# TensorE waits for its own last product at the column groups of four stages

## What is computed

```python
def swiglu(h, w_in, w_out):
    gate, up = jnp.split(h @ w_in, 2, axis=-1)
    return (jax.nn.silu(gate) * up) @ w_out

def sq_relu_mlp(u, w_up, w_down):
    return jnp.square(jax.nn.relu(u @ w_up)) @ w_down

for layer in range(2):
    x = x + 0.5 * swiglu(rmsnorm(x, ffn1_norm[layer]), ffn1_w_in[layer], ffn1_w_out[layer])
    ...
    x = x + 0.5 * swiglu(rmsnorm(x, ffn2_norm[layer]), ffn2_w_in[layer], ffn2_w_out[layer])
for i in range(4):
    ...
    h = h + rmsnorm_2(sq_relu_mlp(u, mlp_w_up[i], mlp_w_down[i]), norm_gains[i, 3])
```

## Time and profile before

| | |
|---|---|
| median of 3 runs | 2801.15 us (2799.4 to 2806.18) |
| the profiled execution | 2810.09 us |
| its span, first to last instruction | 2808.3 us |
| TensorE products / weight loads, share of the span | 96% / 93% |
| VectorE, ScalarE | 65%, 50% |
| mean share of the transfer engines' time | 48.8% |
| mean granted TensorE clock | 0.992 of full speed |

### The profile page before, as it was taken

The page is one execution under the profiler, slowest core; times in us unless marked ns, Lnnn a source line. Parts: engine busy times, 40 slices in busy tenths (PEclk is TensorE's granted clock), DMA queues, the critical chain, the costliest instruction groups (busy, mean ns, idle before and its releaser), DMA issues. The chain is left out here.

```text
span 2808.3 us, 49234 instructions
## 1 busy us (share of the span) xinstructions
PE 2706.5 (96%) x21106; PEld 2609.7 (93%) x21106; DVE 1817.8 (65%) x2364; ACT 1410.7 (50%) x1928; POOL 0.2 (0%) x4
## 2 busy tenths in 40 slices
PE   8999999999998899999999999989999899999998
PEld 8998999999987889999899999879988899989998
DVE  6658666656657746666656755967455685656764
ACT  5445654454466354545445465354454544446443
POOL 0000000000000000000000000000000000000000
PEclk9999999999999999999999999999999999999999
DMA  6554546555534234655544554135542465454463
GB/s 240 173 183 141 185 138 195 187 185 188 188 122 123 76 123 133 200 186 175 177 134 154 181 195 151 61 114 181 191 149 91 148 195 195 152 171 150 151 198 133
DMA packets 129865, 450.12 MB, mean 160 GB/s; under 512 B 20208, under 2 KB 21104, under 8 KB 129520
## 3 DMA queue, kind: packets, MB, share of 16 engines
q1 hardware_dynamic: 129504, 446.83, 48.8%
q10 hardware_dynamic: 144, 0.14, 0.0%
HBM read 445.48 MB, written 1.44 MB: 159 GB/s over the span
## 5 line engine op out<-in xcount | busy, mean ns | idle before, releaser
L266 PE MATMUL B<-R,WH 128*128 128x256 f32 x10432 | 2088.0, 283 | 37.6 <-DVE WL L980 23.4
L266 PEld LDWEIGHTS B<-R,WH 128*128 128x128 f32 x10432 | 1675.3, 189 | 57.1 <-DVE WL L980 25.0
L980 DVE TENSOR_TENSOR WL<-SL,WH 128x1024 fp32r<-128x1024 f32 x835 | 1010.4, 1223 | 755.0 <-ACT WH L2037 753.9
L266 PE MATMUL B<-R,WL 128*128 128x256 f32 x4480 | 1254.9, 280 | 0.0
L2037 ACT ACTIVATE WH<-SL 128x1024 fp32r<-128x1024 f32 x835 | 866.1, 1053 | 585.5 <-PE B L266 458.2
L266 PEld LDWEIGHTS B<-R,WL 128*128 128x128 f32 x4480 | 846.7, 189 | 0.0
L266 PE MATMUL B<-RB,WH 128*128 128x256 f32 x1984 | 555.5, 280 | 1.8 <-DVE WL L980 1.8
L266 PE MATMUL B<-RB,WL 128*128 128x256 f32 x1728 | 482.3, 279 | 0.0
L266 PEld LDWEIGHTS B<-RB,WH 128*128 128x128 f32 x1984 | 372.2, 188 | 2.5 <-DVE WL L980 2.2
L266 PEld LDWEIGHTS B<-RB,WL 128*128 128x128 f32 x1728 | 324.4, 188 | 0.0
L266 PE MATMUL B<-WH,R 128*128 128x512 f32 x480 | 159.2, 401 | 1.1 <-DVE WL L980 1.1
(11 more groups left out here) (287 smaller groups left out, 1583.0 us busy)
## 6 DMA issues: line engine op xcount, KB each, us to landing
SL<-in_w SPq DMA_DIRECT2D x835, 512.0 KB, 3.5
CP<-in_cp SPq DMA_DIRECT2D x5, 768.0 KB, 6.6
PG<-in_mem SPq DMA_DIRECT2D x1, 1024.0 KB, 7.1
PK<-in_pk SPq DMA_DIRECT2D x1, 594.5 KB, 7.1
XG<-in_xT SPq DMA_DIRECT2D x1, 512.0 KB, 7.7
out<-XG SPq DMA_DIRECT2D x1, 512.0 KB, 2.6
SL<-in_w SPq DMA_DIRECT2D x1, 384.0 KB, 3.5
XG<-in_xT SPq DMA_DIRECT2D x1, 256.0 KB, 6.1
```

What stands on the lines that cost most here:

```text
L266: return p.matmul(o, left, right, start=first, stop=final, skip_group_check=True)
L980: v.tensor_tensor(WL[t % NSPL][:, :], SL[t % NRAW][:, :], WH[t % NSPL][:, :].bitcast(F32), ALU.subtract).then_inc(s_lo, 1)
```

## The change

Two waits of TensorE for itself are added, nothing is taken away.

In f2.0.in (groups 1 to 21) and m0.up (groups 1 to 15), ahead of the group's first block, TensorE waits until `s_block` has reached the number of that block, i.e. until its own last product is done. In m0.up the first blocks of groups 1 and 2 are the second and third block of the stage.

In f1.1.in and f2.1.in (groups 1 to 21) it waits for the bank of the next small product, issues one more product of the group's weights (128 columns of them) with the first 16 + 2j columns of the activations into that bank, and waits for it on a semaphore of its own. What it writes is read by nobody, and the bank's turn isn't moved on.

```diff
+        own_mm = Tally(sem("s_own_mm"))
...
             def tile(st, j, k):
                 b = st.at(j, k)
+                if k == 0 and st.name in ("f2.0.in", "m0.up") and j:
+                    p.wait_ge(s_block, b)
                 if b == 0:
                     p.wait_ge(s_lo_first, 1)
                 elif b == 1 or b % 4 == 0:
...
             def multiply(st, j, k, xh, xl, lower=None):
                 hi, lo, at = tile(st, j, k)
+                if k == 0 and st.name in ("f1.1.in", "f2.1.in") and j:
+                    x = len(took)
+                    p.wait_ge(s_bank[4 + x % 3], x // 3)
+                    mm(BK[4 + x % 3][:, 0:16 + 2 * j], hi[:, at:at + 128], xh[:, 0:16 + 2 * j]).then_inc(own_mm.sem, own_mm.up())
+                    p.wait_ge(own_mm.sem, own_mm.n)
                 if k == 0 and st.used(j):
                     p.wait_ge(s_bank[st.bank(j)], st.used(j))
                 bk = BK[st.bank(j)]
```

## The result

The changed kernel takes 2834.49 us, the median of four runs (2829.59 to 2838.34), beside 2803.06 us for four runs of the kernel before (2799.4 to 2806.18): a ratio of 1.0112, with a 95% interval of 1.0089 to 1.0134. That is 31.4 us more, where the forecast was 24.6, and 8.8 us above the forecast time of 2825.7, inside the range of 2818 to 2840. The profiled execution of the changed kernel took 2829.59 us, 2827.8 of them its span.

The account below looks back on a forecast made before the run. TensorE, 96% busy, was taken to bound the kernel nearly everywhere. Thirty exposed waits (9.8 us) and 42 short products with waits (14.8 us) add 24.6 us to 2801.15, giving 2825.7 us, range 2818 to 2840.

Parts of the forecast that it names:

- The pure wait: In f2.0.in and m0.up, each exposed wait on s_block costs 0.326 us; 30 of them cost 9.8 us.
- the upper one: Upper bound for the signal from product end to weight load: 0.13 us, against 0.055 taken.
- The six hidden ones: Group 1 of f2.0.in and five waits in m0.up cost nothing, covered by other stalls; uncovered they cost 2.0 us.
- The short product: In f1.1.in and f2.1.in, each short product with its wait costs 0.352 us; 42 of them cost 14.8 us.
- four passes: If so narrow a product ran in four passes of 38 columns: 0.048 us more each, 2.0 us in all.
- The clock did not fall: Rival: the clock falls in the touched stages, giving 2847 or 2976 us; chance 0.07 of adding over 12 us.
- The weight load is held: Rival: TensorE loads the next weights before the wait ends, 0.105 us less per wait, 2818 us; chance 0.07.
- The low stretches did not vanish: Rival: half-clock stretches outside the four stages vanish, giving back 18 us, 2807 us, not slower; chance 0.04.
- The waits do what they say: Rival: the waited values were already reached, so 2801 us for waits alone, 2806 with short products; chance 0.02.
- nothing else changes: Nothing is removed or moved, and all stages other than the four touched ones stay as before.
- the base of the sum: The median of the runs of the kernel before, 2801.15 us, to which 24.6 us was added.
- the bounds alone: Total time from the terms' low and high values, without the spread of the runs: 2824 to 2835 us.

Follow-up runs that it names:

- e1_again: The changed kernel once more, with no edit; 2827.99 us, ratio 1.0104 to the kernel before.
- e2_only_a: The changed kernel with only the waits on s_block in f2.0.in and m0.up, no short products; 2811.10 us, ratio 1.0041 to the kernel before.
- e10_chain4: The changed kernel without the s_block waits, four short products with a wait each in place of one per group; 2853.65 us, a single run.
- e7: The changed kernel without short products, each s_block wait for one block less; 2800.86 us, a single run.
- e8: The changed kernel without short products, each s_block wait in an instruction of its own ahead of the weight load; 2811.92 us, a single run.
- e9: The changed kernel without s_block waits, short products held at 80 then 82 columns in f1.1.in, 92 then 104 in f2.1.in; 2807.55 us, a single run.
- e3: The changed kernel with only the short products and their waits in f1.1.in and f2.1.in; 2815.26 us, ratio 1.0063 to the kernel before.
- e4_b_no_wait: The changed kernel with only the short products, TensorE not waiting for them, and no s_block waits; 2804.16 us, ratio 1.0019 to the kernel before.
- e5_one_late: The changed kernel without short products, its s_block waits replaced by one ahead of group 8 of each .up stage; 2806.56 us, ratio 1.0001 to before.

## Why the prediction was right, and where it was not

**The pure wait.** Forecast 0.326 us; measured 0.324 as 6.47 / 20 in f2.0.in. The release is 0.33 us behind the product's start, and 0.05 behind its recorded end, as taken from the earlier trace rows. For a product of 256 columns the modelled end served as well as a true one. The value taken, near the low end of its bounds, was right, and the upper one had no case: even the wait in an instruction of its own cost 0.34 to 0.35, not 0.40. The 0.13 us of the earlier trace rows are the way from VectorE through a separate instruction to a load of ONES, and they were a bound only because no nearer row was there.

**The six hidden ones.** Shown for f2.0.in, where 20 prices fill the 6.47 us and 21 would be 6.8. m0.up is less clean: 2.18 us more than before's trace, forecast 3.3. But that trace had the stage 0.9 us longer than those with no waits and the slow beat (98.33, 98.36, 98.45). Against 98.36 the changed kernel has 3.07, e1_again 3.18 and e2_only_a 3.45, where ten waits are 3.2 and fifteen would be 4.8. That the waits ahead of the gaps only shorten them can be read off the changed kernel's products in the first part of m0.up:

```profile
PE B L267 <- DVE WL L988: 0.6, 1, 0.6
...
PE B L267 <- DVE PG L1037: 0.5, 1, 0.5
...
PE B L267 <- ACT PG L2179: 0.5, 1, 0.5
```

One wait for WL of 0.6 us is left there, where the earlier trace rows has 2.3 us in three. (The 1.1 us of the second line of the earlier trace rows is the last of these three, whose product runs over the edge of both windows; the prediction names it as if it were a fourth. No sum hangs on it.) The time TensorE loses to itself it doesn't lose to VectorE.

**The short product.** Forecast 0.352 us; measured 0.360. The slot was right: the short product starts 0.118 us behind the one ahead. The step that went wrong is the release. I took the recorded duration of the earlier trace rows for the time to the end, let it grow by 0.42 ns a column from 0.179 to 0.196, and added 0.055, as if nothing ran ahead of the short product: the load would be released 0.234 to 0.251 us after the product's start. It is released after 0.252 us at every width from 20 to 58, so 1 to 18 ns later, in the mean 10, which with a slot and a restart 1 ns shorter each is the 0.008 by which the term was too small. The record was not to blame. In e10_chain4, where nothing is in flight ahead, each load comes 0.057 us behind the recorded end at 20 columns and at 58, just as the prediction had it; behind a wide product the release is held to 0.252 us up to some 76 columns. What holds it was not separated: the wide product's own release is due 0.333 us after its start, 0.215 after that of the short one. (The Trainium skill, "Perfetto Trace Analysis", section on the Tensor Engine instruction, says that this end is worked out from the instruction's size; the traces agree, since the record grows by 16 ns from 20 to 58 columns, whether the release follows it, as in the chain, or stands still, as behind a wide product.) That a product might run in four passes had no case.

**The rivals.** The clock did not fall: 1.00 in all touched stretches, and also with four short products and waits in a row (e10_chain4). (The Trainium skill, "TensorE: Matmul & The Clock Gate", section on a second HAM failure mode, tells of a kernel whose clock goes to and fro by small pauses between groups; the waits here, one in 6 us, and the chains of four short products, 1.3 us in every 7, did not do it.) The weight load is held: it starts 0.05 us or more behind the recorded end of the waited product each time and never before. The low stretches did not vanish, 34.1 us in place of 37.5, and they differ from trace to trace, from 23.9 to 44.4, with no relation to the edit that shows. The waits do what they say.

**The rest of the sum.** The direct price by the measured terms is 30 x 0.323 + 42 x 0.360 = 24.8 us (the two prices by the length of a group, less 48 slots). Forecast 24.6. The runs say 31.4 (24.9 to 37.6) and 29.1 (23.8 to 34.7), so 4 to 7 us seem to be missing. One part of it may be the step "nothing else changes". In the changed kernel's two traces only one restart behind an own wait went from the slow beat to the quick one, and the quick stretch of f1.1.in that it began came to its end at the next own wait. The loads of groups 1 to 4 of f1.1.in in the changed kernel:

```profile
611.79 0.30 PEld L267 LDWEIGHTS B<-R,WH 128*128 128x128 f32 x2 [0.28 <-PE B L267]
...
617.60 0.30 PEld L267 LDWEIGHTS B<-R,WH 128*128 128x128 f32 x2 [0.18 <-PE B L267]
...
623.61 0.30 PEld L267 LDWEIGHTS B<-R,WH 128*128 128x128 f32 x2 [0.18 <-PE B L267]
...
629.63 0.30 PEld L267 LDWEIGHTS B<-R,WH 128*128 128x128 f32 x2 [0.18 <-PE B L267]
```

5.81 us, then 6.01 and 6.02. Over all the traces a quick beat ahead of a waited short product was lost in 36 of 38 cases; ahead of a wide own wait on the weight load it stood only once, and was lost. A kernel without such waits can win the quick beat for a whole stage: f2.0.in came out of its first stall with it in 3 of 12 traces (e7, e8, e9; the two with rows of short products left out), worth 6.8 us with f2.0.out, and m0.up with m0.dn in one of seven (e3), 6.4 us less than in the trace of before. The changed kernel did so in neither of its traces. That is 6.8 / 4 + 6.4 / 7 = 2.6 us on average, an estimate from few traces and argued, not shown, and 24.8 + 2.6 = 27.4 us lies within both intervals, as 24.8 does within the second. Whether the last 2 to 4 us are anything more than spread stays open: the stages without an edit, 2316.4 us in before and 2312.4 in after, point the other way in the one pair of traces.

**The base and the range.** The runs shown beside the changed kernel put before at 2803.06, 1.9 us above the base of the sum. The time lies in the range and just under the end of 2835 that the bounds alone gave, but by none of what that end was made of: no signal of 0.13 us, no four passes, and the six stayed hidden. The sum of the waits was right by its mechanism; that the whole came out inside the range, 4 to 7 us above that sum, is in part luck.

## What to carry to other kernels

A wait of TensorE for its own last product is the product's latency plus the restart, less the three slots that would have run: a third of a microsecond, whatever the size of the stage, and it can be put together from a product's duration, any signal and any restart of the trace. It costs nothing where TensorE is about to stall for something else, and nothing if it waits for a product six places further back. A narrow product that is waited for behind a wide one costs as much as one of 76 columns. When two kernels differ by a few us more or less than the sum says, count products per microsecond in gap-free stretches at full clock before looking for a cause in the edit.

## What the runs showed of the hardware that was not expected

**Two beats at one clock.** With TensorE fed without a gap and the granted clock at 1.00, products of 128 x 128 by 128 x 256 start every 0.1178 us or every 0.1133 us, 4% apart. One of the two lasts from one stall of TensorE to the next, over some 180 us and some 1,580 products in e7_one_early (418.8 to 598.4) and across a stage's border, and a restart can change it. A stall isn't needed for that: in e4_b_no_wait a short product without a wait ended the quick beat of group 1 of f2.1.in. Behind a wait for its own wide product, on the weight load, it was the slow one every time, but where the beat ahead can be told, it had been slow before in all cases but one; in an instruction of its own the beat ahead was kept (32 of 32); behind a waited short product a quick beat was lost in 36 of 38 cases, and a slow one turned quick in 38 of 249, most often at 80 columns; and behind VectorE's WL it was now and then the quick one. A difference of nanoseconds in the distance from product to load may decide it, but no run here shows the rule.

**A floor behind a wide product.** A product of 20 to 76 columns that starts 0.118 us behind a wide one releases its waiter 0.251 to 0.254 us after its start, though its record says 0.17 to 0.20 and grows with the columns. With nothing in flight ahead (e10_chain4) the release follows the record, 0.057 us behind its end, and takes 0.43 ns a column.

**A quick beat can end at a late WL.** In e5_one_late the quick stretch of m1.up ran into a wait for WL and came out of it slow. The weight load of this kernel that ends the stretch:

```profile
1952.24 0.30 PEld L267 LDWEIGHTS B<-R,WH 128*128 128x128 f32 x2 [0.61 <-DVE WL L983]
```

How much of the gain is given back in that way was not measured.
